# Two transformer blocks in one launch: layer C's wide softmax blocks are scaled and turned by one matrix product with a diagonal, and the compressed keys lie on a block diagonal

## The reference, cut to what matters

```python
def block(args):                       # 128 queries at a time
    i, qb, gb = args
    t = i * Q_BLOCK + jnp.arange(Q_BLOCK)
    s_c = jnp.einsum('bqghd,bngd->bghqn', qb, kc) * scale
    p_c = masked_softmax(s_c, cmp_end[None, :] <= t[:, None])
    o_c = jnp.einsum('bghqn,bngd->bqghd', p_c.astype(vc.dtype), vc)
    ...
    s_s = jnp.einsum('bqghd,bgqkd->bghqk', qb, k_g) * scale
    p_s = masked_softmax(s_s, valid_s[:, :, None]).astype(v_g.dtype)
    o_s = jnp.einsum('bghqk,bgqkd->bqghd', p_s, v_g)
    ...
    s_w = jnp.einsum('bqghd,bkgd->bghqk', qb, kw) * scale
    p_w = masked_softmax(s_w, valid_w).astype(vw.dtype)
    o_w = jnp.einsum('bghqk,bkgd->bqghd', p_w, vw)
    out = gb[..., 0:1] * o_c + gb[..., 1:2] * o_s + gb[..., 2:3] * o_w
```

## Time and profile before

| what | value |
|---|---|
| median of 3 runs | 2537.54 us (2537.01 to 2543.62) |
| the profiled execution | 2534.34 us, span 2533.0 us |
| PE busy in the span | 2307.1 us (91%) |
| DVE busy | 1427.5 us (56%) |
| ACT busy | 539.9 us (21%) |
| PE busy from 946 to 1160 us | 179.33 of 214.00 us |
| DVE busy there | 183.36 us |
| ACT busy there | 105.63 us |

### The profile page before, as it was taken

The page is one execution under the profiler, slowest core; times in us unless marked ns, Lnnn a source line. Parts: engine busy times, 40 slices in busy tenths (PEclk is TensorE's granted clock), DMA queues, the critical chain, the costliest instruction groups (busy, mean ns, idle before and its releaser), DMA issues.

```text
span 2533.0 us, 29573 instructions
## 1 busy us (share of the span) xinstructions
PE 2307.1 (91%) x10920; PEld 1680.7 (66%) x10920; DVE 1427.5 (56%) x3707; ACT 539.9 (21%) x1325; POOL 65.9 (3%) x67
## 2 busy tenths in 40 slices
PE   8997889999999978889999999998889688988887
PEld 6864578888888864547888888885566533333332
DVE  6559867656656538887666566664756411111114
ACT  2013342101002015542110011103454211111111
POOL 0000000000000000000000000000000011111110
PEclk9998799999999968999999999998699899999999
DMA  5212002232224300001322223222003499999996
GB/s 206 91 50 67 1 18 84 84 93 91 84 83 153 99 18 1 1 1 51 92 92 83 83 91 93 84 84 87 1 1 135 169 357 419 419 419 419 419 420 289
DMA packets 69455, 350.18 MB, mean 138 GB/s; under 512 B 10804, under 2 KB 11060, under 8 KB 43776
## 3 DMA queue, kind: packets, MB, share of 16 engines
q1 hardware_dynamic: 64144, 339.18, 36.2%
q0 software_dynamic: 4880, 8.05, 0.9%
q10 hardware_dynamic: 288, 1.05, 0.1%
HBM read 343.05 MB, written 17.30 MB: 142 GB/s over the span
## 4 chain that ended last, share of the span: by engine, by line
PE 66%; DVE 9%; DMA 7%; ACT 3%; issue 2%; SPq 0%; DVEq 0%; POOLq 0%
PE bank L549 24%; PE bank L562 7%; PE bank L552 7%; PE bank L557 7%; PE bank L2253 6%; DMA w<-in_experts 6%; PE bank L2261 4%; PE bank L540 2%; DVE exps L1678 1%; PE bank L751 1%; DVE exps L1849 1%; PE bank L2229 1%; DMA y_pairs<-oN,idx 1%; PE bank L821 1%; PE bank L971 1%
## 5 line engine op out<-in xcount | busy, mean ns | idle before, releaser
L2253 PE MATMUL bank<-w,xT 128*64 128x512 f32 x1024 | 230.5, 598 | 9.1 <-DMA w<-in_experts 8.4
L2416 DVE COPY square<-bank 128x256 f32<-128x256 f32 x32 | 13.6, 425 | 354.3 <-ACT rope L2347 354.3
L2253 PEld LDWEIGHTS bank<-w,xT 128*64 128x64 f32 x1024 | 71.9, 138 | 162.4 <-issue 134.0
L1204 ACT ACTIVATE exps<-exps,small 128x128 f32<-128x128 f32 (+1 forms) x224 | 123.9, 554 | 183.9 <-DVE small L1678 183.9
L1449 DVE TENSOR_TENSOR third<-first,bank 128x256 f32<-128x256 f32 x108 | 45.5, 421 | 175.1 <-PE bank L549 174.4
L549 PE MATMUL bank<-u,ring 128*128 128x256 f32 x608 | 143.6, 379 | 0.0
L2261 PE MATMUL bank<-w,square 128*64 128x512 f32 x512 | 135.8, 679 | 2.1 <-ACT square L2354 2.1
L549 PEld LDWEIGHTS bank<-u,ring 128*128 128x128 f32 x608 | 115.5, 190 | 15.7
L549 PE MATMUL bank<-h_sums,w_sum 128*128 128x256 f32 x512 | 121.0, 379 | 0.0
L549 PE MATMUL bank<-h,ring 128*128 128x256 f32 x512 | 121.0, 379 | 0.0
L549 PE MATMUL bank<-u_mlp,ring 128*128 128x256 f32 x480 | 113.4, 379 | 0.0
(11 more groups left out here) (447 smaller groups left out, 4283.7 us busy)
## 6 DMA issues: line engine op xcount, KB each, us to landing
w<-in_experts SPq DMA_DIRECT2D x192, 1024.0 KB, 27.6
ring<-in_dense SPq DMA_DIRECT2D x216, 512.0 KB, 3.8
w<-y_pairs SPq DMA_DIRECT2D x4, 1024.0 KB, 26.8
consts<-in_consts SPq DMA_DIRECT2D x1, 2054.5 KB, 16.5
x<-in_xT SPq DMA_DIRECT2D x4, 512.0 KB, 7.8
cmp_v<-in_cmp_v SPq DMA_DIRECT2D x1, 2048.0 KB
cmp_k<-in_cmp_k SPq DMA_DIRECT2D x1, 2048.0 KB
h_tokens<-w SPq DMA_DIRECT2D x4, 512.0 KB, 2.9
```

What stands on the lines that cost most here:

```text
L1204: act.activation(e, e, ACT.Exp, bias=neg[:, a:a + 1], scale=-1.0, accum_out=total[:, a:a + 1]).then_inc(s[done], 1)
L2253: ins = k.pe.matmul(bank[a * CAP:(a + 1) * CAP, :], xT[:, kk % 4, kk // 4, :], w[:, (2 * (kk % 2) + a) * EH:(2 * (kk % 2) + a + 1) * EH], ...
```

## The change

For the 32 wide blocks, DVE no longer multiplies the tiles. It still forms the reciprocal times the gate. ACT then writes a 128x128 diagonal matrix for each head: the identity, with each row scaled by that number (`act_nsa_diagonal`, in step n + 2, between the exponentials of block n + 2 and the copy of block n − 1, counted from the wide block n). PE multiplies the unscaled tile by this diagonal, which turns and scales it in one product. The diagonals take eight places in the two `square` buffers, so the ninth waits for the first to be read. The 32 narrow blocks are done as they were.

The compressed keys of both heads are kept on a block diagonal, `k_cmp` of 128 by 64 with zeros off the blocks. The compressed logits of a pair become four products of 128 rows by 64 keys, without the wait in their middle, and DVE reads them with one instruction. `k_cmp` is zeroed once and filled by two copies instead of one.

```diff
+        k.diag = [sq[:, P * i:P * (i + 1)] for sq in k.sqp for i in range(4)]
...
+DIAGONAL = [n for n, (m, x, b) in enumerate(NSA) if b >= 2]
+NTH = {n: i for i, n in enumerate(DIAGONAL)}
...
+def diagonal(k, n, a):
+    return k.diag[(2 * NTH[n] + a) % 8]
...
 def pe_nsa_turn(k, n):
     for a in range(2):
-        pe.wait_ge(s["c_scaled"], 2 * n + a + 1)
+        if n in NTH:
+            pe.wait_ge(s["c_diagonal"], 2 * NTH[n] + a + 1)
+        else:
+            pe.wait_ge(s["c_scaled"], 2 * (n - len([i for i in DIAGONAL if i < n])) + a + 1)
...
         for j in range(b + 1):
-            ins = pe.transpose(k.bank[4 + a][:, j * P:(j + 1) * P], e[:, j * P:(j + 1) * P], k.const("ident"))
+            out, src = k.bank[4 + a][:, j * P:(j + 1) * P], e[:, j * P:(j + 1) * P]
+            if n in NTH:
+                ins = pe.matmul(out, src, diagonal(k, n, a), start=True, stop=True)
+            else:
+                ins = pe.transpose(out, src, k.const("ident"))
...
 def pe_cmp_logits(k, m):
-    for a in range(2):
-        r = slice(a * HD, (a + 1) * HD)
-        if a:
-            pe.wait_ge(s["cmp_half"], m + 1)
-        for b in range(NB):
-            ins = pe.matmul(ch.bank[:, a * P + b * 32:a * P + (b + 1) * 32], k.yc[r, m, b * P:(b + 1) * P], k.kc[r, :],
-                            start=True, stop=True)
-        if a == 0:
-            ins.then_inc(s["cmp_half"], 1)
+    for b in range(NB):
+        ins = pe.matmul(ch.bank[:, b * 64:(b + 1) * 64], k.yc[:, m, b * P:(b + 1) * P], k.kc.rearrange("p a n -> p (a n)"),
+                        start=True, stop=True)
...
     (act_nsa, after the exponentials of the step)
+        if step - 2 in NTH:
+            act_nsa_diagonal(k, step - 2)
...
+def act_nsa_diagonal(k, n):
+    act, s, i = k.act, k.s, NTH[n]
+    neg, total, inv = soft_columns(k, n)
+    act.wait_ge(s["c_inv"], i + 1)
+    for a in range(2):
+        if i >= 4:
+            act.wait_ge(s["c_t_done"], 2 * DIAGONAL[i - 4] + a + 1)
+        act.activation(diagonal(k, n, a), k.const("ident"), ACT.Copy, scale=inv[:, a:a + 1]).then_inc(s["c_diagonal"], 1)
...
 def dve_nsa_scale(k, n):
+    if n in NTH:
+        gated.then_inc(s["c_inv"], 1)
+        return
...
 def dve_cmp_logits(k, m):
-    for a in range(2):
-        ins = dve.scalar_tensor_tensor(pc[:, a::2, :], k.ch7.bank[:, a * P:(a + 1) * P].rearrange("p (b n) -> p b n", n=32), SCALE,
-                                       add[:, :, a, :], ALU.mult, ALU.add)
-    ins.then_inc(k.ch7.emptied, 1)
+    dve.scalar_tensor_tensor(pc.rearrange("p a n -> p (a n)"), k.ch7.bank[:, 0:2 * P], SCALE, k.const("cmp_add"),
+                             ALU.mult, ALU.add).then_inc(k.ch7.emptied, 1)
```

More of the change, by code:

```diff
@@ L290, in signals @@
     s.new("lg_done", "masked", "exp_done", "t_done", "turned0", "turned1")
-    s.new("c_lg_done", "c_masked", "c_exp_done", "c_scaled", "c_t_done", "c_turned0", "c_turned1", "c_weighed")
+    s.new("c_lg_done", "c_masked", "c_exp_done", "c_scaled", "c_inv", "c_diagonal", "c_t_done", "c_turned0", "c_turned1", "c_weighed")
     s.new("gates_exp", "cmp_k_in", "cmp_v_in", "cmp_2_in", "win_zero")
-    s.new("win_v", "win_k", "hid_z", "hid_exp", "hid_ready", "cmp_half", "cmp_shifted", "cmp_exp", "cmp_weights")
+    s.new("win_v", "win_k", "hid_z", "hid_exp", "hid_ready", "cmp_shifted", "cmp_exp", "cmp_weights")
     s.new("zeroed", "row_out", "bias_in", "lam_dot", "lam_exp", "qk_normed")
@@ L356, in buffers @@
         k.hz = sb("hid_z", [P, 4, 32], stack=st)
-        k.kc = sb("k_cmp", [P, 32], stack=st)
+        k.kc = sb("k_cmp", [P, 2, 32], stack=st)
         k.rep = sb("hid_rep", [P, 4, 32], stack=st)
@@ L829, in pe_cmp_logits @@
 def pe_cmp_logits(k, m):
-    pe, s, ch = k.pe, k.s, k.ch7
+    pe, ch = k.pe, k.ch7
     pe.wait_ge(ch.emptied, ch.n)
-    for a in range(2):
-        r = slice(a * HD, (a + 1) * HD)
-        if a:
-            pe.wait_ge(s["cmp_half"], m + 1)
-        for b in range(NB):
-            ins = pe.matmul(ch.bank[:, a * P + b * 32:a * P + (b + 1) * 32], k.yc[r, m, b * P:(b + 1) * P], k.kc[r, :],
-                            start=True, stop=True)
-        if a == 0:
-            ins.then_inc(s["cmp_half"], 1)
+    for b in range(NB):
+        ins = pe.matmul(ch.bank[:, b * 64:(b + 1) * 64], k.yc[:, m, b * P:(b + 1) * P], k.kc.rearrange("p a n -> p (a n)"),
+                        start=True, stop=True)
     ch.end(ins, ("cmp", m))
@@ L1785, in dve_c_prepare @@
     own.link(dve.memset(k.vcd, 0.0))
+    diagonal = own.link(dve.memset(k.kc, 0.0))
     flat = lambda v: v.rearrange("p a n -> p (a n)")
@@ L1803, in dve_c_prepare @@
     dve.tensor_copy(k.rep[:, 2:4], hid[:, 2:4]).then_inc(s["hid_ready"], 1)
-    dve_take(k, k.ch6, "k_cmp", k.kc, k.ch6.bank[:, 0:32])
+    dve.wait_ge(own.sem, diagonal)
+    dve.wait_ge(k.ch6.filled, k.ch6.at["k_cmp"])
+    dve.tensor_copy(k.kc[0:HD, 0, :], k.ch6.bank[0:HD, 0:32])
+    dve.tensor_copy(k.kc[HD:P, 1, :], k.ch6.bank[HD:P, 0:32]).then_inc(k.ch6.emptied, 1)
     dve.wait_ge(k.ch7.filled, k.ch7.at["v_cmp"])
@@ L1845, in dve_nsa_scale @@
     dve.wait_ge(own.sem, own.link(dve.reciprocal(inv, total)))
-    dve.wait_ge(own.sem, own.link(dve.tensor_tensor(inv, inv, k.gt[:, b, 6 * m + 1 + x:6 * m + 6:3], ALU.mult)))
+    gated = dve.tensor_tensor(inv, inv, k.gt[:, b, 6 * m + 1 + x:6 * m + 6:3], ALU.mult)
+    if n in NTH:
+        gated.then_inc(s["c_inv"], 1)
+        return
+    dve.wait_ge(own.sem, own.link(gated))
     for a in range(2):
@@ L1868, in dve_cmp_logits @@
     mx, sm = cmp_columns(k, m)
-    add = k.const("cmp_add").rearrange("p (b a n) -> p b a n", a=2, n=32)
     dve.wait_ge(k.ch7.filled, k.ch7.at["cmp", m])
-    for a in range(2):
-        ins = dve.scalar_tensor_tensor(pc[:, a::2, :], k.ch7.bank[:, a * P:(a + 1) * P].rearrange("p (b n) -> p b n", n=32), SCALE,
-                                       add[:, :, a, :], ALU.mult, ALU.add)
-    ins.then_inc(k.ch7.emptied, 1)
+    dve.scalar_tensor_tensor(pc.rearrange("p a n -> p (a n)"), k.ch7.bank[:, 0:2 * P], SCALE, k.const("cmp_add"),
+                             ALU.mult, ALU.add).then_inc(k.ch7.emptied, 1)
     dve.wait_ge(k.ch7.emptied, k.ch7.at["cmp", m])
```

## The result

The changed kernel takes 2546.85 us (median of 7 runs, 2544.72 to 2554.42), the kernel before 2537.01 us in its 7. The medians lie 9.8 us apart. The ratio is 1.0044, 95% interval 1.0026 to 1.0062, which is 11 us slower (6.6 to 15.7), where 4.5 us faster was forecast and 2541 us was the top of the range.

The account below looks back on a forecast made before the run. No engine was full; a serial chain through PE, DVE and ACT set the period. Seven periods gave −5.2 us, first pair +0.3, drain +0.4: −4.5 us, 2533 us as median, range 2522 to 2541.

Parts of the forecast that it names:

- the sentence behind the sum of the loop: PE at full clock throughout the loop, without stretches at 1.2 GHz: about 1.5 to 2 of the 5.2 us gained.
- The rival with the drops: Half-clock stretches stay, with PE now on the path; each costs up to 1 us: 2536 us, 12%.
- my loop: Chain from one turn of place 6 to the next, in five steps: 24.85 us a period against 25.44.
- step 4: PE from the turn of place 2 through the compressed logits, without a pause; sum 21.95 us; added products fill earlier standstills.
- the product costs two transposes: PE's wide blocks: 0.226 us a product against 0.117 a transpose, adding 3.2 us a pair, 25 in all.
- the chain on DVE and ACT of 1.38 us: Step 5, after the compressed logits: from DVE's start to ACT's exponential, 1.38 us.
- the 5.04 us from DVE's copy to the turn of place 1: Step 2: DVE's copy of bank 5, compressed weights, mask, ACT's exponentials and copy; 5.04 us, unchanged.
- The first pair: Start of the loop, at half clock until about 963 us: fewer small records but dearer products, +0.3 us.
- the drain: After the last period: two products' turns lie bare, +1.6 us, less 1.2 for the multiplications: +0.4.
- DVE sets the pace after all: Loop waits shorter than assumed, PE's own work the floor at 21.3 us a pair; half that gain, 14 us: 2523, 23%.
- The clock comes up with the first products: First pair at full clock from about 960.8 us instead of 963: 2532 us, 15%.
- The products are slower than L860's: Wide turns load a fresh tile for each product; at 0.15 us a record, 10 us slower: 2547, 10%.

Follow-up runs that it names:

- e3: The changed kernel with two unread products of 512 columns filling PE's pause ahead of the turn of place 6: 2546.34 us, ratio 1.0039 to the kernel before.
- e2: The changed kernel with the compressed keys, their logits and DVE's two instructions as before, so diagonals alone: 2560.37 us, ratio 1.0106 to the kernel before.
- e4: The changed kernel with fourteen unread 128x128 transposes filling PE's pause ahead of the turn of place 6: 2539.53 us, ratio 1.0028 to the kernel before.
- e9: The changed kernel with the compressed softmax moved later and ACT's copy of bank 4 ahead of the diagonals: 2524.58 us, ratio 0.9947 to the kernel before.
- e1: The kernel before with the block-diagonal compressed keys alone, without products by diagonals: 2523.38 us, ratio 0.9962 to the kernel before.
- e11: The kernel before with the block-diagonal keys alone, the same kernel run again: 2525.16 us, ratio 0.9955 to the kernel before.
- e10: The kernel before with block-diagonal keys, plus two unread scaled identities written by ACT for each wide block: 2531.93 us, ratio 0.9977 to the kernel before.
- e6: The changed kernel with DVE's part of the compressed softmax and ACT's exponential of it moved from place 0 to place 1: 2529.54 us, ratio 0.9956 to the kernel before.

## Why the prediction was wrong

**The step that failed is the clock, in the sentence behind the sum of the loop:** "PE stalls less, so the stretches at 1.2 GHz should not come", and with it the gain of 1.5 to 2 us for the drops of before. PE stalled less in total, 3.3 us a round for 4.1 to 4.8, but longer in one place, 1.73 us instead of 1.07, and the half clock came in every period. By the timeline's starts, from the turn of place 6 to the logits took 2.58 us, from there to the turn of place 7 1.37, 3.95 in all; at full clock the same two distances are 1.51 and 0.84 in e2 (1010.85 to 1013.20). So a drop cost 1.6 us a pair, 11.2 in seven. e3 and e4, 1.6 us a round shorter with the pause filled, say the same. The time that I gave the drops, 0.5 us a period, was taken from a kernel where PE waited 4 to 5 us a round; here little of a drop is hidden. The rival with the drops had the right mechanism and a price (up to 1 us each, 2536) that was too low by more than a third, on a forecast that already stood too low.

**The second error is a sum of small ones.** The rest of my loop was 0.9 us a pair short, 6.2 in all: its distances on PE came out up to 0.15 longer than I had them, such as 1.51 for 1.36 and 0.84 for 0.75 in the two just named, 1.42 for 1.36 and 1.89 for 1.81 in the turns of places 2 and 3, 0.95 for 0.86 in the rope, 2.73 for 2.62 from the values to the compressed logits. I had made them of durations less an assumed overlap, each a little too generous. −5.2 + 11.2 + 6.2 is the +12.2 that the seven periods show. With all of that and no drop, the seven periods would have been 1 us longer than before, so the forecast's 5.2 us were not there even at full clock. One reading of rows was wrong too: step 4 has PE standing still ahead of 1040.38, but in the earlier trace rows it works through from 1038.74 to 1042; only the 1.43 us ahead of 1045.70 were free for the added products.

**What held:** the product costs two transposes, not four (16 records in 2.05 us); the diagonal 0.39 us and 0.58 for two; the compressed logits 1.14 us to DVE; the chain on DVE and ACT of 1.38 us; the 5.04 us from DVE's copy to the turn of place 1 (1036.76 to 1041.80); the pauses of 1.73 and 0.62 us (1.8 and 0.6 forecast); DVE's freed time going into a wait for PE. The first pair took 22.28 us (22.53 before, +0.3 forecast), the drain 10.44 (9.26 before, +1.2 for +0.4). Neither decides.

**The rivals:** "DVE sets the pace after all" did not come true for the change: DVE's relief alone gained nothing. e9 reached 23.77 a pair for 25.44, but with two moves that the change does not have. "The clock comes up with the first products" is not what happened: in the first pair of the changed kernel the clock was back at 1.00 from 962.7 us, 964.0 before, while e1 and e11, which turn with transposes, had it from 966.6 and 960.1, so the change lies within what kernels without such products show. "The products are slower than L860's": 0.118 a record for 0.113, far from 0.144; it gave the right side for the wrong reason. (By its own sum, 4.5 over 392 records, the gain would be gone at 0.125, not at 0.123.)

Open is what decides between a drop and none at a given pause: 1.07 us brought four in seven periods before, 1.15 none in e1, 1.66 sometimes none in e2, 1.73 three in e10 and seven in the change. Two drops of e2 began with PE at work. One rival to the length of the pause is its moment. In the change the seven drops begin 27.3 us apart, as long as a round with a drop lasts, so each falls on the turn of place 6 again; in e10, with the same pauses and another round, they do not. No run shifts a pause in time and leaves the rest as it is, so that every round had a drop may be luck of this round's length.

## What to carry to other kernels

When a change takes work from one engine and hands it to others, ask first where the new instructions stand in their engines' order: with the products, two short writes ahead of a copy took part in turning a gain into a loss (alone, in e10, they cost nothing at full clock), and moving them and one softmax recovered it. Where TensorE pauses for a microsecond or two in each round, price the pause with the half clock that may come after it, on the path as it will be, and don't count on a busier TensorE to prevent it. Split a change that has two parts: here one gained 10 us and the other lost 23.

## What the runs showed of the hardware

In the change, pauses of 1.73 us in a loop where PE is busy 22.7 of 26 us went with 3.4 us at the 1.2 GHz level in each of seven rounds; in e10, where PE is busy 19 of 24.5 us, the same pauses did in three. Useless work in the pause removed it and made the round 1.6 us shorter. Fourteen transposes served for this as well as four records of 512 columns. Pauses of 0.93 and 0.62 us, 1.5 us apart, had a drop behind them once in e4, once in e6 and three times in e2, and none in the other rounds of these kernels. Two drops of e2 began after 5.4 us in which PE was busy 5.37. A 128x128 fp32 product took the time of two transposes, 1.58 us for six (12 records) against 0.85 for six transposes.
